# The gates of the 64 decode tokens by scattered additions instead of one-hot products

## What is computed

```python
q = (xn @ w_q).reshape(bsz, t, P_HEADS, 2, P_QDIM // 2)            # 8 heads
s = jnp.einsum('bthcd,ckd->bthck', q, sub_keys)                    # 128 sub-keys a side
sv, si = lax.top_k(s, P_TOPK)                                      # 16 a side, then 16 of the 256 pairs
eid = jnp.take_along_axis(cand_id, top_pos, axis=-1)               # expert = 128 * side 0 + side 1
gate = jax.nn.softmax(top_s, axis=-1)
hid = jnp.einsum('td,ted->te', xb, u_tab[eb])                      # only the 128 experts that a token picked
out = jnp.einsum('te,ted->td', jax.nn.gelu(hid) * gb, v_tab[eb])
```

## Time and profile before

| what | value |
|---|---|
| median of 3 runs | 2195.39 us (2193.57 to 2197.99) |
| profiled execution | 2195.33 us, its span 2193.5 us |
| TensorE busy | 2109.4 us, 96% of the span |
| VectorE, ScalarE, GpSimd busy | 1319.1, 869.8, 983.9 us |
| spreading stage | from 922.6 to 1104 us of the span |
| granted TensorE clock, mean | 0.98 of full speed |

### The profile page before, as it was taken

How to read it: one execution, slowest core, us unless ns; L and a number is a source line. 1 busy time by engine, 2 the same in 40 slices (tenths; PEclk the granted TensorE clock), 3 DMA queues, 4 the chain that set the end, 5 groups by cost and what they waited for, 6 DMA issues and landing times.

```text
span 2193.5 us, 41955 instructions
## 1 busy us (share of the span) xinstructions
PE 2109.4 (96%) x16647; PEld 2054.5 (94%) x16647; DVE 1319.1 (60%) x2502; ACT 869.8 (40%) x1693; POOL 983.9 (45%) x619
## 2 busy tenths in 40 slices
PE   8997898898999999999999999999999999999997
PEld 7996787788999999999999999999999999999996
DVE  4564656667778988699811111111257787777776
ACT  5334455543333333499832222222233333333332
POOL 1433344422254554411133333333367787777620
PEclk9999999999999999999999999999999999999998
DMA  3447267625465666477776767676669999999972
GB/s 129 179 137 218 88 190 222 189 81 184 137 197 191 192 194 198 131 210 224 224 256 237 253 219 237 239 250 215 221 239 337 336 336 340 339 339 330 334 267 77
DMA packets 302135, 488.98 MB, mean 223 GB/s; under 512 B 34400, under 2 KB 226720, under 8 KB 301832
## 3 DMA queue, kind: packets, MB, share of 16 engines
q1 hardware_dynamic: 273800, 402.55, 55.5%
q0 software_dynamic: 28160, 83.99, 11.1%
HBM read 395.61 MB, written 157.50 MB: 252 GB/s over the span
## 4 chain that ended last, share of the span: by engine, by line
PE 71%; DVE 2%; ACT 1%; DMA 1%; issue 1%; SPq 0%; POOL 0%; DVEq 0%; ACTq 0%; POOLq 0%
PE banks L130 22%; PE banks L131 22%; PE banks L132 22%; PE banks L2299 4%; PE banks L1975 1%; DMA u_raw<-arg_u 1%; DVE n_y L349 0%; DMA scratch_hid<-gelu_ahead 0%; SPq L2163 0%; DVE res_x L2846 0%; DVE res_lo L356 0%; DVE n_sq L390 0%; DVE n_inv L342 0%; DVE gates_in L2853 0%; DVE gates_in L2843 0%
## 5 line engine op out<-in xcount | busy, mean ns | idle before, releaser
L130 PE MATMUL banks<-res_hi,u_high 128*128 128x288 f32 x1456 | 438.4, 301 | 4.2 <-POOL u_low L2172 3.2
L132 PE MATMUL banks<-res_hi,u_low 128*128 128x288 f32 x1456 | 429.6, 295 | 0.0
L131 PE MATMUL banks<-res_lo,u_high 128*128 128x288 f32 x1456 | 429.6, 295 | 0.0
L130 PE MATMUL banks<-w_high,v_high 128*128 128x416 f32 x1024 | 360.0, 352 | 0.3 <-DVE w_low L2727 0.3
L131 PE MATMUL banks<-w_low,v_high 128*128 128x416 f32 x1024 | 359.3, 351 | 0.0
L132 PE MATMUL banks<-w_high,v_low 128*128 128x416 f32 x1024 | 357.2, 349 | 0.0
L2172 POOL TENSOR_TENSOR u_low<-u_raw,u_high 128x1024 fp32r<-128x1024 f32 x75 | 179.9, 2399 | 306.0 <-ACT u_high L2168 306.0
L2734 DVE TENSOR_TENSOR gated<-gelu_out,gates_in 128x416 f32<-128x416 f32 x76 | 44.9, 592 | 418.9 <-ACT gelu_out L2688 385.4
L130 PEld LDWEIGHTS banks<-res_hi,u_high 128*128 128x128 f32 x1456 | 274.2, 188 | 4.9 <-POOL u_low L2172 3.7
L131 PEld LDWEIGHTS banks<-res_lo,u_high 128*128 128x128 f32 x1456 | 274.2, 188 | 0.1
L132 PEld LDWEIGHTS banks<-res_hi,u_low 128*128 128x128 f32 x1456 | 273.8, 188 | 0.0
(11 more groups left out here) (443 smaller groups left out, 4535.0 us busy)
## 6 DMA issues: line engine op xcount, KB each, us to landing
scratch_v_rows<-arg_v SPq DMA_DIRECT2D x128, 512.0 KB, 7.5
v_raw<-scratch_v_rows SPq DMA_DIRECT2D x128, 512.0 KB, 6.1
u_raw<-arg_u SPq DMA_DIRECT2D x37, 1024.0 KB, 5.7
scratch_gates<-gate_stage SPq DMA_DIRECT2D x13, 2048.0 KB, 9.4
scratch_prod<-gated SPq DMA_DIRECT2D x128, 208.0 KB, 3.3
w_raw<-scratch_prod SPq DMA_DIRECT2D x128, 208.0 KB, 5.0
q_raw<-arg_u SPq DMA_DIRECT2D x38, 512.0 KB, 3.9
gates_in<-scratch_gates SPq DMA_DIRECT2D x19, 832.0 KB, 5.0
```

The costliest lines, as they stand in the source:

```text
L130: pe.matmul(out, ah, bh, start=first, stop=False)
L131: pe.matmul(out, ah, bl, start=False, stop=False)
L132: return pe.matmul(out, al, bh, start=False, stop=last)
```

## The change

The table gets a second part, `LastGates.dst`, for the last 64 tokens. It is zeroed by one transfer of 4 MB from a zeroed tile while routing begins. When the picks are known, VectorE computes each pick's place in it (`place_last`), SyncE deals places and gates over 128 partitions (`deal`: 64 tokens by two halves), and GpSimd adds them with 64 indirect transfers of 128 single elements each (`scatter`), one for each head and half-pick. Before the first one of a head it waits until all those before have landed. The 64 are put between and behind the 12 `low` operations of `pool_spread`: after the n-th, those up to `n * 64 // 12`, so 5 or 6 each time, and 6 after the last one, ahead of the count that TensorE waits for. Spreading is left with 352 tokens (`SPREAD_N`), 6 steps and 12 keys; two more keys become jobs of routing (`AHEAD4` 40), so 14 key jobs behind the last tile of `w_q`. Every load of gates becomes two. SyncE and GpSimd wait in `gates_stored` for the scattered additions as well.

```diff
@@ -74,10 +74,13 @@
 SP = P + REST
 DN = TOK - SP
 NB = DN // TB
-G_STEPS = -(-DN // (2 * TB))
+DEC_NB = DEC_SEQ // TB
+SPREAD_N = DN - DEC_SEQ
+SPREAD_NB = SPREAD_N // TB
+G_STEPS = -(-SPREAD_N // (2 * TB))
 EARLY = 3
 AHEAD5 = 2 * G_STEPS
-AHEAD4 = 38
+AHEAD4 = 40
 NH = NG - (AHEAD4 + AHEAD5) // JJ
 KEY4, KEY5 = NH * JJ, NH * JJ + AHEAD4
@@ -162,7 +165,7 @@
         self.v_rows = VRows(self)
         self.hid = nc.dram_tensor("scratch_hid", (N_KEYS, P, SP), F32, kind="Internal").ap()
         self.prod = nc.dram_tensor("scratch_prod", (N_KEYS, P, DN), F32, kind="Internal").ap()
-        self.gates = a["gates"].rearrange("g p t j -> g p (t j)")[:, :, 0:DN * JJ].rearrange(
+        self.gates = a["gates"].rearrange("g p t j -> g p (t j)")[:, :, 0:SPREAD_N * JJ].rearrange(
             "g p (n j t) -> g p n j t", j=JJ, t=TB)
         self.chains = {name: Chain(self.sem(name + "_chain")) for name in ("pe", "act", "pool", "dve")}
@@ -214,6 +217,51 @@
     def ready(self, eng):
         eng.wait_ge(self.copied, 16 * N_KEYS)
+class LastGates:
+    HALF_K = TOPK // 2
+    COUNT = P_HEADS * HALF_K
+    def __init__(self, core, ctx):
+        self.dst = core.nc.dram_tensor("scratch_last_gates", (NG, P, DEC_NB, JJ, TB), F32, kind="Internal").ap()
+        self.zeros = core.sb("gate_zeros", [P, DEC_NB * JJ * TB], ctx=ctx)
+        self.all_place = core.sb("last_place", [P, SEL], U32, ctx=ctx)
+        self.all_gate = core.sb("last_gate", [P, SEL], ctx=ctx)
+        self.place = core.sb("place_by_half", [P, P_HEADS, self.HALF_K], U32, ctx=ctx)
+        self.gate = core.sb("gate_by_half", [P, P_HEADS, self.HALF_K], ctx=ctx)
+        self.made, self.zeroed = core.sem("gate_zeros_made"), core.sem("last_gates_zeroed")
+        self.placed, self.dealt, self.done = core.sem("last_placed"), core.sem("last_dealt"), core.sem("last_scattered")
+    def zero(self, sp):
+        sp.wait_ge(self.made, 1)
+        sp.dma_start(self.dst.rearrange("g p n j t -> p g (n j t)"),
+                     bc(self.zeros[:, :], 1, [P, NG, DEC_NB * JJ * TB])).then_inc(self.zeroed, 16)
+    def deal(self, sp):
+        sp.wait_ge(self.placed, 2)
+        for whole, half in ((self.all_place, self.place), (self.all_gate, self.gate)):
+            src = whole[0:DEC_SEQ, :].rearrange("p (h b k) -> p h b k", b=2, k=self.HALF_K)
+            for b in range(2):
+                sp.dma_start(half[b * DEC_SEQ:(b + 1) * DEC_SEQ, :, :], src[:, :, b, :]).then_inc(self.dealt, 16)
+    def scatter(self, pool, n):
+        h, k = n // self.HALF_K, n % self.HALF_K
+        if n == 0:
+            pool.wait_ge(self.dealt, 64)
+            pool.wait_ge(self.zeroed, 16)
+        elif k == 0:
+            pool.wait_ge(self.done, 16 * n)
+        pool.indirect_dma_start(
+            out=self.dst.rearrange("g p n j t -> (g p n j t)").unsqueeze(1),
+            out_offset=bass.IndirectOffsetOnAxis(ap=self.place[:, h, k:k + 1], axis=0),
+            in_=self.gate[:, h, k:k + 1], in_offset=None, compute_op=ALU.add).then_inc(self.done, 16)
+    def ready(self, eng):
+        eng.wait_ge(self.done, 16 * self.COUNT)
 class Sparse:
...
@@ -1922,6 +1970,7 @@
         rkf = sb("pick_rank_f", P, 2, NT, TOPK)
         gsum = sb("gate_sum", P, NT, 2)
         picks = sb("picks", P, NT, 3, SEL)
+        cut = sb("last_key_parts", P, 2, SEL, dt=U32)
         par_in = core.sem("route_in")
         s_done, s_taken = core.sem("scores_done"), core.sem("scores_taken")
         ranked, zeroed = core.sem("ranked"), core.sem("scores_zeroed")
@@ -1934,6 +1983,7 @@
             sp.dma_start(keys[:, :, :], a["keysT"]).then_inc(par_in, 16)
             sp.dma_start(numbers[:, :], a["ranks"]).then_inc(par_in, 16)
             spread.first_load(sp)
+            last.zero(sp)
             def send(j):
                 kind, n = jobs[j]
                 if kind == "hidden":
@@ -1953,6 +2003,7 @@
         def pool_route(pool, spread):
             pool.memset(sc[:, :, NT - 1, :], 0.0).then_inc(zeroed, 1)
+            pool.memset(last.zeros[:, :], 0.0).then_inc(last.made, 1)
             def match_keys(h, side):
                 pool.wait_ge(matched, 2 * h + side + 1)
@@ -2110,6 +2161,24 @@
                 dve.tensor_copy(sparse.hidden[:, REST_SEL:], left[:, 2, :]).then_inc(sparse.ready, 1)
                 dve.tensor_copy(sparse.gate[:, REST_SEL:], picks[:, 0, 2, :]).then_inc(sparse.ready, 1)
+            def place_last():
+                n = NT - 1
+                link(dve.tensor_scalar(gsum[:, 1, 0:1], gsum[:, 0, 0:1], float(TB), float((JJ - 1) * TB), ALU.is_ge, ALU.mult))
+                dve.tensor_tensor(gsum[:, 1, 1:2], gsum[:, 1, 0:1], gsum[:, 0, 0:1], ALU.add)
+                dve.tensor_copy(last.all_gate[:, :], picks[:, n, 2, :]).then_inc(last.placed, 1)
+                link(dve.tensor_copy(cut[:, 0, :], picks[:, n, 1, :]))
+                link(dve.tensor_scalar(cut[:, 1, :], cut[:, 0, :], JJ - 1, None, ALU.bitwise_and))
+                dve.tensor_copy(left[:, 0, :], cut[:, 1, :])
+                link(dve.scalar_tensor_tensor(out=left[:, 1, :], in0=picks[:, n, 1, :], scalar=float(P // JJ),
+                                              in1=picks[:, n, 0, :], op0=ALU.mult, op1=ALU.add))
+                pitch = DEC_NB * JJ * TB
+                link(dve.tensor_scalar(left[:, 2, :], left[:, 1, :], float(pitch), gsum[:, 1, 1:2], ALU.mult, ALU.add))
+                link(dve.scalar_tensor_tensor(out=left[:, 3, :], in0=left[:, 0, :], scalar=float(TB - P * pitch // JJ),
+                                              in1=left[:, 2, :], op0=ALU.mult, op1=ALU.add))
+                dve.tensor_copy(last.all_place[:, :], left[:, 3, :]).then_inc(last.placed, 1)
             norm.dve_half(dve, 1)
             dve.wait_ge(par_in, 32)
             for h in range(P_HEADS):
@@ -2140,6 +2209,8 @@
                 dve.wait_ge(matched, 2 * h + 2)
             finish_picks(P_HEADS - 1)
             place_picks()
+            dve.wait_ge(sparse.ready, 6)
+            place_last()
     return Route(sp_route, pool_route, pe_route, act_route, dve_route)
...
@@ -2199,7 +2270,7 @@
         LEAD = 2
         TAKE = {PER: {4: (0, 0), 8: (0, 1), 12: (1, 0), 15: (1, 1)}, PER // 2: {2: (0, 0), 4: (0, 1), 6: (1, 0), 7: (1, 1)}}
         SPLIT = {PER: {2: (1, 0), 9: (0, 1)}, PER // 2: {1: (1, 0), 4: (0, 1)}}
-        LAST_PER = (DN - (steps - 1) * 2 * TB) // FOUR
+        LAST_PER = (SPREAD_N - (steps - 1) * 2 * TB) // FOUR
         ALL_G = (steps - 1) * PER + LAST_PER
         uh, ul = u.hi, u.lo
         u_in = [core.sem(f"u_ahead_in{n}") for n in range(2)]
@@ -2240,6 +2311,7 @@
                 sp.dma_start(u.raw[:, 0, 0], a["u"][0]).then_inc(u_in[0], 16)
                 sp.dma_start(u.raw[:, 0, 1], a["u"][1]).then_inc(u.loaded[0], 16)
+            last.deal(sp)
             for n in range(2):
                 sp.wait_ge(gelu_sent_ahead[n], 32 * (AHEAD4 // 2))
             with sp.Fori(0, steps - 1) as it:
@@ -2265,9 +2337,12 @@
             low(pool, 0, 0)
         def pool_spread(pool):
-            with pool.Fori(0, steps) as it:
-                low(pool, it, 1)
-                low(pool, it + 1, 0)
+            begun = 0
+            for n in range(1, 2 * steps + 1):
+                low(pool, n // 2, n % 2)
+                for m in range(begun, n * last.COUNT // (2 * steps)):
+                    last.scatter(pool, m)
+                begun = n * last.COUNT // (2 * steps)
             pool.wait_ge(u_low, 2 * steps + 3)
             pool.sem_inc(u.low, 1)
             u.split_low(pool, 0, 1)
@@ -2402,6 +2477,7 @@
             step(steps - 1, True)
     def gates_stored(eng):
+        last.ready(eng)
         for b in range(2):
             eng.wait_ge(sent[b], 16 * (steps + 1 if LAST_PER > 8 * b else steps))
             eng.wait_ge(gelu_sent[b], 32 * (steps + 1))
...
@@ -2521,7 +2597,8 @@
         def load_gates(sp, buf, sems, g, q):
-            sp.dma_start(buf[:, q % 2], core.gates[g]).then_inc(sems[q % 2], 16)
+            sp.dma_start(buf[:, q % 2, 0:SPREAD_NB], core.gates[g]).then_inc(sems[q % 2], 16)
+            sp.dma_start(buf[:, q % 2, SPREAD_NB:], last.dst[g]).then_inc(sems[q % 2], 16)
         def load_v(sp, k):
             if k >= V_SLOTS:
@@ -2738,13 +2815,13 @@
                 g, jj = n // JJ, n % JJ
                 dve.wait_ge(gelu_done, n + 1)
                 if jj == 0:
-                    dve.wait_ge(gc_in[g % 2], 16 * (g // 2 + 1))
+                    dve.wait_ge(gc_in[g % 2], 32 * (g // 2 + 1))
                 make(dve, n, gelu[:, n % G_SLOTS, cols], gates_c[:, g % 2, :, jj, :])
                 for e in todo.made_at(n):
                     q = e // JJ
                     dve.wait_ge(he_in[e % H_SLOTS], 16 * (e // H_SLOTS + 1))
                     if e % JJ == 0:
-                        dve.wait_ge(ge_in[q % 2], 16 * (q // 2 + 1))
+                        dve.wait_ge(ge_in[q % 2], 32 * (q // 2 + 1))
```

(13 more changed lines are left out.)

## The result

The changed kernel is slower: 2219.76 us, median of 4 runs (2215.43 to 2240.36), against 2194.48 for the kernel before (4 runs, 2190.51 to 2197.99). The ratio is 1.0112, 95% interval 1.0078 to 1.0146, so 25 us more, where 8.5 less were forecast and 2204 was the upper end. The profiled execution took 2215.43 us, its span 2213.6, against 2193.5 before: 20.1 us more.

The account below looks back on a forecast made before the run. TensorE, busy 96% of the span, was taken to bound the kernel. -14.3 us of its work plus 5.8 of tail gave -8.5 against 2195.33: 2186.8 us, own range 2183 to 2191, 8-in-10 range 2181 to 2204.

Parts of the forecast that it names:

- Taken away: Spreading loses one step of 27.01 us, routing gains two keys, 12.72 us: net 14.29 us less TensorE work.
- Hidden in routing: Zeroing, clearing, places and dealing in routing cost nothing, up to 3 us if the zeroes take their upper bound.
- The scattered additions: GpSimd in spreading: 1.4 us a scatter, 1.25 where VectorE is idle, 5.5 us to land, priced from gathers.
- 23 of 27 us: GpSimd's load per spreading step: 19.8 us of work plus 3 us of landing waits, within TensorE's 27.
- So nothing reaches TensorE until the last step: In spreading, low parts end some 4.5 us before TensorE needs them, so no wait before the last step.
- The four landing waits inside batches: GpSimd waits 4.1 us for a landing inside a batch at four heads of the seven, 3 us a step.
- The tail: End of spreading, ahead of key 0: TensorE stalls 9.0 us, 3.2 given back, so it costs 5.8 us.
- The 3.2 us: Hidden stage: TensorE's old idle times ahead of keys 2 and 4, 1.82 and 1.38 us, go.
- GpSimd becomes the bound: Rival in spreading: 1.7 us a scatter, 9 to land, 28.3 us a step, stall 34 us, 2212; chance 0.27.
- VectorE becomes the bound: Rival in spreading: scatters hold up VectorE's one-input operation, 8.6 us a step, +32 us, 2227; chance 0.09.
- The tail is hidden: Rival at spreading's end: 11th batch doesn't delay key 0's low part, stall 3.7 us, 2181.6; chance 0.06.
- upper bound of 2.3 us: Highest price of a scatter, 2.03 + 0.30; with 5.5 us to land, the stall is 42 us.

Follow-up runs that it names:

- e1: Changed kernel without its 64 scattered additions, clearing, zeroing, dealing and doubled loads kept: ratio to the kernel before 0.9940, medians 2193.41 and 2206.57 us.
- e3: Changed kernel with its 64 scatters writing plainly instead of adding, all waits kept: ratio to the kernel before 0.9931, stage 200.2 us.
- e7: Changed kernel with scattered additions for the last 32 tokens only, 32 transfers, spreading 384 tokens: 2185.56 us against 2199.46 before, ratio 0.9935.
- e8: Changed kernel with 32 additions for the last 32 tokens, none behind key 0's low part: ratio to the kernel before 0.9928, stage 198.0 us.
- e9: Changed kernel once more without any edit, on another chip: ratio to the kernel before 1.0075, stage 229.2 us.
- e4: Changed kernel with the count that releases key 0 put ahead of the last batch of six additions: ratio to the kernel before 1.0089, stage 232.6 us.
- e5: Changed kernel with each head's additions into a table of its own, so none waits for another's landing: ratio to the kernel before 1.0012, stage 215.4 us.
- e6: Changed kernel with the count and key 1's low part both ahead of the last six additions: ratio to the kernel before 1.0077, stage 228.9 us.

## Why the prediction was wrong

**Taken away: right.** 88 groups, and routing grew by 12.7 us for two keys. The firm term of -14.3 us stands.

**Hidden in routing: right.** The zeroes took 14.8 us to land (15 taken), SyncE's loads behind them were late, and TensorE was busy for 30.00 of the 30 us from 570 on. e1 has all of this, and its median is 13.2 us below that of before on the same chip.

**The scattered additions: here it failed.** The step of the prediction is "So I take 1.4 us a scatter there and 1.25 where VectorE is idle", with 5.5 us for the landing. Measured: 2.24 us with issue in the mean of all 64, 1.86 (1.55 and 0.30) where VectorE is idle, and 7.2 to 8.3 us to land at three of the four heads that stand inside a batch. All of it came from rows of gathers. For a plain scatter those rows were right: e3 shows 0.962 and 0.957 at least, against 0.947 and 0.940. It was the addition that had no row. The lower bound of 1.24 was also no bound, since no addition of this kernel took less than 1.86. "23 of 27 us" of GpSimd's step was 31.7: from the first `low`, at 940.82, to the one of key 0, at 1114.98, it needed 174.2 us for 5.5 steps, for which TensorE needs 148.6. Of these 25.6 us the six waits passed 18.8 on to TensorE; the other 6.8 went into the lead that GpSimd had at first and into TensorE's own slower clock.

**"So nothing reaches TensorE until the last step": wrong by that.** 18.8 us reached it within the steps, which the prediction itself had named as a sign that it is wrong. The four landing waits inside batches were foreseen, with 16.4 us in all (4 x 4.1), and took 18.6; it was the price of the additions that used up the room.

**The tail: right place, larger.** TensorE waited for the count 12.3 us. Before, it waited 1.03 us there for ScalarE, so 11.3 us were added, not 9.0. From the start of key 0's low part to the count the forecast has 9.8 us (1104.2 to 1114.0). Measured are 13.2 (1114.98 to 1128.16), as the sum of three misses: the pause of 5.39 us ahead of the third addition; six additions at 1.86 instead of 1.25, 3.7 more; and 5.9 less, because the count was let through at 1128.16 and not behind the last addition, which ended at 1134.05. TensorE was ready 0.85 us after that `low` began (at 1128.16 - 12.33 = 1115.83), which takes 1.0 us of its wait away against the forecast. That the sum comes near the 9.0 is partly luck. The 3.2 us were given back: TensorE waits ahead of no later key up to 1180.

Put together: 31.1 us of waits, less the 1.0 of before and the 3.2, are 26.9 of the 34.9. The clock explains most of the rest. In stretches of 3 us the granted clock is 0.50, the lower of its two levels (1.2 GHz), at 1025 to 1028 and at 1076 to 1079, behind TensorE's two long waits, and back at 1.00 from 1031 and from 1082 on. TensorE's busy time, each stretch times the share of the clock that is missing, gives some 6.5 us ahead of key 0 and 1.9 behind it, where the dip of the earlier trace rows had 1.7: an estimate of 6.7 us more than before. Some 1.3 us stay unexplained.

**The rivals.** *GpSimd becomes the bound* is what happened: low parts late, and a slower kernel. It expected a stall of 34 us; 31.1 were measured as waits and 34.9 as a whole. That these agree so well is luck: it took 1.7 us for an addition and 9 for each landing, where 2.24 and 3.3 to 8.3 were measured. It had a chance of 0.27, and against it stood "128 elements of 4 bytes are little": they are few bytes, but 144 packets. Whether the packets are what costs GpSimd its time is not shown. *VectorE becomes the bound* is refuted. Its one-input operation beside the additions (ns min/median/max) was not slowed:

```profile
L2470 DVE TENSOR_SCALAR onehot_pairs<-numbers,cur_keys,cur_gates x88: 328/336/385, 931.2 to 1104.9; 128x128 f32<-128x128 f32 x88
```

before it took 329/334/344, and TensorE waited for VectorE's pairs for 0.3 us in all, as before. *The tail is hidden* came true only with half the additions (e7, e8).

**The range.** My own upper bound of 2.3 us for one addition gave a stall of 42 us, so some 2220 us (-14.3 + 42 - 3.2), and it stood in the text as a rival's variant while the range ended at 2204. The measured price was 2.24. An operation that no row showed had been given the price of its nearest row, and outcomes that need that price had been given 0.64. The prediction's sentence on a landing in 2.0 us, after the Trainium skill (DMA: Bandwidth & Descriptors, Anatomy of one DMA), reckons 2.5 us for what is 3.5 (5.5 less 2.0). The shortest landing of an addition that the changed kernel's chain shows took 3.3 us. e3 also warns against reading too much into agreement: its stage of 200.2 us is what the forecast would give (194.5 + 5.8), but that is luck too, for it has 2.1 us of wait for the count, 3.2 for low parts and 2.9 for one-hot products and their issue, not 9.0 less 3.2.

**Open.** Ahead of the third addition of the last batch GpSimd stands for 5.4 to 8.0 us with no releaser shown, in the changed kernel, its repetition e9, e4, e5 and e6 alike. In all five the first loads of the hidden stage run then. They alone don't do it: in e3 the plain writes of the last batch (from 1102.17 us) run beside the same loads (from 1101.17) without a pause. What holds GpSimd was not tried. So how much of the loss at the end is the price of the additions and how much this pause stays open. The 18.8 us within the steps don't depend on it. Nor was it tried whether two table halves, so that heads alternate, would keep the 64 additions' landing waits away; by e5 it would not be enough.

## What to carry to other kernels

A plain row for an operation is no price for its accumulating form: where the trace shows only the one, run one of the other, or let the range reach to the price at which the helper engine sets the pace. Add up the helper's time per step with issue and landing waits included, and compare it with the step of the engine that it feeds. Below that line its work was free here (32 additions); above it, of 18.6 us of landing waits in GpSimd's time 14.0 were paid in the stage (64 additions, e5). Moving the late work of such an engine past one consumer handed the wait to the next, twice (e4, e6); taking work from it helped (e7).

## What the runs showed of the hardware

- An indirect transfer of 128 single elements cost GpSimd 0.96 us at the least as a plain write and 1.55 us with an addition, with 32 packets against 144.
- Between 943 and 1110 us of the changed kernel an addition took more than 1.62 us only when it began with 0.4 us or more left of a two-input operation of VectorE: 1.85 us with 0.42 left (1031.49), 2.22 with 0.79 left (957.80), 2.46 with 1.03 left (962.85). That is how the prediction had read the earlier trace rows for a gather. One that began just ahead of such an operation took 1.55 (950.93, with the operation beginning at 951.02), and the operation its usual 1.09.
- An addition landed 7.2 to 8.3 us after its start where the DMA engines were fully busy, and 3.3 us or at most 4.1 us after it where they were mostly idle.
- A `low` behind an addition goes with a longer two-input operation of VectorE than a `low` by itself: 4.20 us for the one below, where the longest before was 3.275. GpSimd and VectorE, by their timelines:

```profile
952.79 2.44 POOL L258 DMA_INDIRECT scratch_last_gates<-gate_by_half,place_by_half  x1 [0.30 <-issue]
954.66 2.97 POOL L2333 TENSOR_TENSOR u_low<-u_raw,u_high 128x1024 fp32r<-128x1024 f32 x1
```

```profile
954.39 4.20 DVE L2467 TENSOR_TENSOR onehot_pairs<-numbers,cur_keys 128x896 f32<-128x896 f32 x1 [0.34 <-PE banks L2374]
```

VectorE began during the addition. The `low` ended at 957.63 and VectorE's operation 0.96 us later; alone it takes 1.08. So it seems to have waited both out.
